# MLA heads' last steps: four gated feature tiles turned in the output bank's free half, out units spread over four steps

## What is computed

```python
o = causal_block_attention(q, k, v).reshape(B, S, E_MLA)   # 16 heads of 128
return (o * jax.nn.silu(g)) @ w_out                        # w_out 2048 x 2048
```

## Time and profile before

| | us |
|---|---|
| runs | 2507.94, 2508.91, 2509.61 |
| median | 2508.91 |
| profiled execution | 2509.81 |
| its span | 2508.0 |
| granted PE clock, mean | 0.998 |

### The profile page before, as it was taken

How to read it: one execution, slowest core, us unless ns; L and a number is a source line. 1 busy time by engine, 2 the same in 40 slices (tenths; PEclk the granted TensorE clock), 3 DMA queues, 4 the chain that set the end, 5 groups by cost and what they waited for, 6 DMA issues and landing times.

```text
span 2508.0 us, 34234 instructions
## 1 busy us (share of the span) xinstructions
PE 2480.3 (99%) x12770; PEld 2119.5 (85%) x12770; DVE 1532.5 (61%) x1820; ACT 1323.8 (53%) x1747; POOL 69.3 (3%) x78
## 2 busy tenths in 40 slices
PE   9999999999999999999999999999999999999998
PEld 8888888888789889778888888887988888888886
DVE  7675757744655555556655655555666667686554
ACT  6444444544656665565755455545555545464443
POOL 0000000010000000010100000100000000000110
PEclk9999999999999999999999999999999999999999
DMA  8666666655556644655675564363566666656663
GB/s 305 194 189 188 184 185 191 204 191 187 166 175 187 185 142 136 217 181 189 185 209 164 143 180 143 104 185 110 156 205 179 189 191 184 187 172 203 195 195 113
DMA packets 234239, 450.64 MB, mean 180 GB/s; under 512 B 15105, under 2 KB 60593, under 8 KB 233100
## 3 DMA queue, kind: packets, MB, share of 16 engines
q1 hardware_dynamic: 230624, 435.94, 56.3%
q0 software_dynamic: 2960, 12.58, 1.5%
q10 hardware_dynamic: 540, 0.60, 0.2%
HBM read 446.35 MB, written 2.69 MB: 179 GB/s over the span
## 4 chain that ended last, share of the span: by engine, by line
PE 97%; DVE 1%; ACT 1%; issue 0%; DMA 0%; SPq 0%; DVEq 0%; ACTq 0%
PE ps L662 23%; PE ps L637 18%; PE ps L639 18%; PE ps L638 18%; PE ps L664 12%; PE ps L595 1%; PE ps L1182 1%; PE ps L1049 0%; PE ps L1170 0%; PE ps L903 0%; PE ps L914 0%; PE ps L915 0%; DVE w_lo L1856 0%; DMA raw<-in_pool_w_in 0%; PE ps L686 0%
## 5 line engine op out<-in xcount | busy, mean ns | idle before, releaser
L1856 DVE TENSOR_TENSOR w_lo<-raw,w_hi 128x1024 fp32r<-128x1024 f32 x852 | 1048.1, 1237 | 743.2 <-ACT w_hi L1249 724.1
L1249 ACT ACTIVATE w_hi<-raw 128x1024 fp32r<-128x1024 f32 x852 | 898.9, 1060 | 940.9 <-PE ps L639 570.9
L662 PE MATMUL ps<-x_hi_lo,w_hi 128*128 128x512 f32 x2336 | 821.3, 394 | 1.7 <-DVE w_lo L1856 1.3
L664 PE MATMUL ps<-x_hi_lo,w_lo 128*128 128x256 f32 x2336 | 660.7, 283 | 0.0
L662 PEld LDWEIGHTS ps<-x_hi_lo,w_hi 128*128 128x128 f32 x2336 | 438.7, 188 | 104.0 <-DVE w_lo L1856 2.3
L637 PE MATMUL ps<-w_hi,x_hi_lo 128*128 128x512 f32 (+3 forms) x1280 | 505.0, 395 | 2.6 <-DVE x_hi_lo L1880 1.3
L639 PE MATMUL ps<-w_hi,x_hi_lo 128*128 128x512 f32 (+3 forms) x1280 | 492.0, 384 | 0.0
L638 PE MATMUL ps<-w_lo,x_hi_lo 128*128 128x512 f32 (+3 forms) x1280 | 491.2, 384 | 0.0
L664 PEld LDWEIGHTS ps<-x_hi_lo,w_lo 128*128 128x128 f32 x2336 | 439.2, 188 | 0.0
L637 PEld LDWEIGHTS ps<-w_hi,x_hi_lo 128*128 128x128 f32 x1280 | 241.1, 188 | 45.3 <-issue 5.2
L639 PEld LDWEIGHTS ps<-w_hi,x_hi_lo 128*128 128x128 f32 x1280 | 240.9, 188 | 43.6
(11 more groups left out here) (344 smaller groups left out, 2148.4 us busy)
## 6 DMA issues: line engine op xcount, KB each, us to landing
raw<-in_w_up SPq DMA_DIRECT2D x160, 512.0 KB, 3.9
raw<-in_pool_w_in SPq DMA_DIRECT2D x128, 512.0 KB, 3.9
raw<-in_w_in SPq DMA_DIRECT2D x96, 480.0 KB, 3.7
raw<-in_w_down SPq DMA_DIRECT2D x76, 512.0 KB, 4.7
raw<-in_pool_w_out SPq DMA_DIRECT2D x64, 512.0 KB, 4.4
raw<-in_ple_w_gate SPq DMA_DIRECT2D x64, 512.0 KB, 3.9
raw<-in_mla_w_in SPq DMA_DIRECT2D x56, 448.0 KB, 3.6
raw<-in_pool_w_group SPq DMA_DIRECT2D x32, 512.0 KB, 4.4
```

The lines of the kernel that those rows point to most:

```text
L662: pe.matmul(bank, w_hi[:, slot, cols], xs[:, k].rearrange("p s n -> p (s n)"), start=k == 0, stop=False, skip_group_check=True)
L664: last = pe.matmul(bank[:, 0:T], w_lo[:, slot, cols], xs[:, k, 0, :], start=False, stop=k == nkt - 1, skip_group_check=True)
L1249: act.activation(w_hi[:, u % RING, :], raw[:, slot, :], ACT.Copy).then_inc(S("w_hi"), 1)
L1856: dve.tensor_tensor(w_lo[:, u % RING, :], raw[:, u % RAW, :], w_hi[:, u % RING, :].bitcast(F32), ALU.subtract)\
```

## The change

Four things change.

- Feature tiles 0 to 3 (groups 0 and 1) are turned one by one, at the end of PE's steps 11 to 14, into the free half of bank O. ACT reads each at the end of its step (semaphore `out_tile_T`), DVE after it (`out_tile`). PE waits for this step's gated head before it turns the tile, and the next step's O matmuls wait for DVE to have read it.
- Out units 0 to 3 stand in PE's steps 15 to 18, one in each, ahead of the O matmuls. Units 0 and 1 wait for the tiles, later ones for groups.
- Groups 2, 3 and 4 are turned in the steps: group 2 in step 16 after the probabilities, group 3 at the end of step 17, group 4 at the end of step 18. Groups 5 and 6 are turned ahead of out unit 4, group 7 ahead of unit 5.
- ACT and DVE prepare a weight unit in each of steps 15 to 18, and it now stands ahead of the group. The loop after the heads begins two groups and two units later.

```diff
@@ PE @@
-            if g == 0:
+            if g == 2:
                 pe.wait_ge(S("at_TE"), HEADS)
-            if g == 1:
+            if g == 3:
                 pe.wait_ge(S("at_L"), HEADS)
-            if g == 2:
+            if g == 4:
                 pe.wait_ge(S("at_PTE"), 4 + HEADS)
-            pe.wait_ge(S("at_done"), 4 + (2 * g + 2 if g < 3 else HEADS))
+            pe.wait_ge(S("at_done"), 4 + (2 * g + 2 if g < 5 else HEADS))
...
-                for g in (3, 4) if k == 4 else (k // 2 + 2,) if 4 < k < 12 else ():
+                for g in {8: (5, 6), 10: (7,)}.get(k, ()):
                     turn(gm, heads_out, g)
-                n = out_first + k // 2
-                pe.wait_ge(S(f"t_free{n % 4}"), n // 4 + 2)
+                if k < 4:
+                    pe.wait_ge(S("out_tile"), k + 2)
+                else:
+                    n = out_first + k // 2 - 2
+                    pe.wait_ge(S(f"t_free{n % 4}"), n // 4 + 2)
...
-                if i in (HEADS, HEADS + 1):
-                    turn(gm, heads_out, i - HEADS)
-                if i == HEADS + 1:
-                    next(out_units)
+                if i == HEADS:
+                    turn(gm, heads_out, 2)
...
                 head_products(min(1, STEP_UNITS[i]))
+                if i >= HEADS - 1:
+                    next(out_units)
                 if i >= 3:
...
                     pe.wait_ge(S("at_done"), 4 + hd)
+                    if OUT_TILES <= i - 1 < OUT_TILES + 4:
+                        pe.wait_ge(S("out_tile"), i - OUT_TILES)
...
                 head_products(max(0, STEP_UNITS[i] - 1))
+                if OUT_TILES <= i < OUT_TILES + 4:
+                    k = i - OUT_TILES
+                    pe.wait_ge(S("at_done"), 4 + i - 2)
+                    for tt in range(2):
+                        last = pe.transpose(O_BANK[:, 256 + tt * 128:384 + tt * 128], gm[:, tt, k * 128:k * 128 + 128], ident)
+                    last.then_inc(S("out_tile_T"), 1)
+                if i in (HEADS + 1, HEADS + 2):
+                    turn(gm, heads_out, i + 2 - HEADS)
             t.add("at", HEADS)
 
         mla_heads()
-        turn(gm, heads_out, 2)
@@ ACT @@
                     last.then_inc(S("at_P"), 1)
+                if i >= HEADS - 1:
+                    hi(1)
                 if i >= HEADS:
-                    group(i - HEADS)
-                if i > HEADS:
-                    hi(1)
+                    group(i + 2 - HEADS)
                 hi(max(0, STEP_UNITS[i] - 1))
+                if OUT_TILES <= i < OUT_TILES + 4:
+                    k = i - OUT_TILES
+                    act.wait_ge(S("out_tile_T"), k + 1)
+                    act.activation(xh[:, k, :], O_BANK[:, 256:512], ACT.Copy).then_inc(S("x_hi"), 1)
@@ DVE @@
                     last.then_inc(S("at_L"), 1)
+                if i >= HEADS - 1:
+                    lo(1)
                 if i >= HEADS:
-                    group(i - HEADS)
-                if i > HEADS:
-                    lo(1)
+                    group(i + 2 - HEADS)
                 lo(max(0, STEP_UNITS[i] - 1))
+                if OUT_TILES <= i < OUT_TILES + 4:
+                    k = i - OUT_TILES
+                    dve.wait_ge(S("x_hi"), t.at("xh", 1))
+                    dve.tensor_tensor(xl[:, k, :], O_BANK[:, 256:512], xh[:, k, :].bitcast(F32), ALU.subtract).then_inc(S("out_tile"), 1)
+                    t.add("xh")
```

More of the change, by code:

```diff
@@ L76 @@
 STEP_UNITS = [2, 3] * 7 + [1] + [0] * 4
+OUT_TILES = 11
 GATE_FIRST = MIN_W - (Q_RANK + KV_RANK - 2 * MIN_W) - ROPE
@@ L1559, in mla_heads @@
         def mla_heads():
-            T_BANK, P_BANK = (TB((t.n["bank"] + b) % 4) for b in (0, 2))
+            T_BANK, P_BANK, O_BANK = (TB((t.n["bank"] + b) % 4) for b in (0, 2, 3))
             for i in range(HEADS + 3):
@@ L1613, in _ @@
         for c in range(NCH):
-            mixer_chunk(chunk(8) if c else first_chunk(early=3, begun=2), 6, c)
+            mixer_chunk(chunk(8) if c else first_chunk(early=5, begun=4), 6, c)
             if c == 0:
@@ L2310, in attention @@
             over_heads(dve, t, parts, step, behind=3, chain=8)
-        first_chunk(early=3, begun=2)
+        first_chunk(early=5, begun=4)
         split_p()
```

## The result

| | median us | runs | lowest to highest | against before |
|---|---|---|---|---|
| before | 2508.39 | 21 | 2507.38 to 2509.61 | |
| after | 2514.36 | 21 | 2511.24 to 2518.14 | 1.0025, 95% interval 1.0019 to 1.0031 |

A forecast was written before the change was run, and what follows sets the result against it. It took TensorE, busy 99% of the span, as the bound, so only its waits and clock count. 2508.91 plus 4.0 of waits plus 1.5 of clock gave 2514.4 us, range 2511.5 to 2516.8.

The forecast's parts named there:

- turns of step 16: PE's turns of Q and K in step 16 wait 0.8 to 0.9 us for ACT's delayed table loads and exponentials.
- out unit 2: In step 17, PE waits 3.0 us for group 2's subtraction, behind logits and a weight unit on DVE.
- out unit 3: In step 18, PE waits 2.2 us for group 3, behind gating and a weight unit on DVE.
- turn of group 5: Just after the steps, PE waits 0.7 us for the last head to be done.
- out unit 4: After the steps, PE waits 1.1 us for group 4's subtraction.
- sum, less 3.8 before: New PE waits of 7.8 us less the 3.8 us present before: 4.0 us longer.
- clock, one fall: TensorE's clock falls once to its lower level near the new pauses, costing 1.5 us; likeliest case, chance 0.35.
- sum of 4.66 us: DVE's path in step 16 from the scores' start through logits, weights and subtraction to PE's start; PE has 1.64 us of work.
- Tiles and O at no cost: Steps 11 to 14: tile turns and following O matmuls cost nothing; step 14 tightest with 0.3 us to spare.
- ACT after step 14: ACT reads the last gate chunk after tile 3, table loads moving too: 7.95 us against PE's 7.05.
- three places named for it: Possible clock falls: scores, turns and 3.0 us wait; O, turns and 2.2 us; O, turns and twice about a microsecond.
- rival without a fall: The clock stays up through the new pauses, only waits count: 2512.9 us, chance 0.32.

The follow-up runs named there:

- first experiment: Changed kernel with VectorE's group subtraction again ahead of the weight unit in steps 16 to 18; 2510.18 us, ratio 1.0006.
- reordered kernel: Changed kernel with DVE's group subtraction before the logits, groups 3 and 4 turned before O, ACT's gate chunk read before tile 3; 2506.57 us, ratio 0.9992.
- half filling: Changed kernel with 6, 4, 1 and 2 unread matmuls in TensorE's pauses; 2512.75 us, and 2511.73 when run again beside the changed kernel.

## Why the prediction was right

It said 2514.4 us; the median is 2514.36. Term by term (the last row from the two profiles near the median):

| wait | predicted | measured |
|---|---|---|
| turns of step 16 | 0.8 to 0.9 | 0.70 |
| out unit 2 | 3.0 | 3.02 |
| out unit 3 | 2.2 | 2.13 |
| turn of group 5 | 0.7 | 0.76 |
| out unit 4 | 1.1 | 0.96 |
| sum, less 3.8 before | 4.0 | 3.8 |
| clock, one fall | 1.5 | 1.54 and 1.55 |

**The queue on DVE.** The sum of 4.66 us from the start of the scores (1016.45) to the out unit (1021.11) held row by row: 1.52 to the logits, then logits and maxima 1.18, weights 1.13, subtraction to start 0.83. Taking the weights from ahead of the subtraction shortened the pause by 1.1 us (first experiment), and putting the subtraction ahead of the logits removed it (reordered kernel). This cause is shown.

**Tiles and O at no cost.** The tile turn at 1005.67 came without a wait, the tile's copy on ACT took 0.39 and DVE's subtraction 0.42. O in steps 15 and 16 no longer waits. POOL's loads came later than forecast (1036.93 for 1021.16 in this slowest execution, 15.8 us where some 9 were said), and nothing on PE waited for them.

**ACT after step 14.** The order and the durations held. ACT's timeline of after beside the earlier trace rows:

```profile
1006.09 0.39 ACT L1599 ACTIVATE x_hi_lo<-ps 128x256 fp32r<-128x256 f32 x1 [2.34 <-PE ps L928]
1006.50 1.28 ACT L1353 ACT_TABLE_LOAD   x1
1007.79 1.16 ACT L1353 ACTIVATE mla_gate<-ps,rstd 128x448 f32<-128x448 f32 x2
...
1009.84 1.28 ACT L1588 ACT_TABLE_LOAD   x1
1011.13 0.40 ACT L1588 ACTIVATE mla_logits<-mla_logits,mla_neg_max 128x128 f32<-128x128 f32 x1
```

Both activations start 0.01 us behind a load of 1.28. With a drain of 1.38 us at each load, as the Trainium skill has it ("ScalarE: Activation LUTs", What ACT_TABLE_LOAD costs), the wait in step 16 would have been above 3 us, by estimate; it was 0.70, so the trace does not agree here either.

**The clock.** The likeliest case was one fall at 1.5 us, and that is what the two profiles near the median show in the steps, in the first of the three places named for it and at that price. Two things were not in it. The falls can be longer than the one of the earlier trace rows: the first of the slowest execution ran on over some 6.8 us, through all of out unit 2 and into O. And their number differs between executions of one kernel: the changed kernel spreads over 6.9 us, the kernel before over 2.2, the half filling over 3.3 and 2.4. The rival without a fall is refuted by three profiles out of three with a fall at the end of the pause of 3.02 us (2.86 idle in the row). The Trainium skill ("TensorE: Matmul & The Clock Gate", Why this matters for your kernels) asks only that pauses longer than about this one be avoided. These profiles do not agree with it, but the pause lies at the edge of what it allows; the fall behind pauses of 0.58 and 0.86 us disagrees more clearly.

**Where it was lucky.** The forecast added 5.5 us to 2508.91, the median of three executions; the median of 21 is 2508.39 and the difference 6.0. A start 0.5 too high and a difference 0.5 too small cancel, so the agreement to 0.1 us is chance; to a microsecond it is not. The terms themselves close between profiles: 3.8 of waits and 1.5 of clock make 5.3, and the two profiles near the median stand 5.4 and 4.7 us above that of before (2515.18 and 2514.54 against 2509.81). Between medians 0.7 is left over. A likely reason, not shown: the profile of before contains the later fall and lies 1.4 above its median, so a common execution of before may well be without it, while all three profiles of the changed kernel have it. No profile of before without it exists to settle this. The same kind of remainder stands with no fall in these steps, in the first experiment: waits of 4.8 us against 3.8 give 1.0 and the medians differ by 2.0.

## What to carry to other kernels

When a unit of work is moved forward to fill a gap, follow its inputs through the queue of every engine that makes them: here the filling needed a subtraction that stood behind the very logits that the step itself produces last, plus the unit's own weights, and each filled gap of 0.7 to 1.5 us became a pause of 2 to 3. Price such a pause with the clock that falls behind it, another 1.5 us on 3.8 in this case, and compare several profiles before taking the number of falls as the kernel's. Two remedies reached the same time here. One is the order of the queues: the operation that the bounding engine waits for goes first on the other engines (2506.57 with four units in the steps). The other is to move only the units whose inputs are ready (2506.70 with two, once ACT's order was mended too).

## What the runs showed of the hardware that was not expected

- A matmul of float32 operands, 128x128 against 256 columns, stands in the trace as two and takes 0.42 us back to back (12 of them 4.99), where a 512-column matmul of the rounded type takes 0.23 to 0.24 (12 of them 2.87).
- With unread matmuls in the pauses the granted clock was 1.00 through the steps in three profiles (in two of them 2.5 us of filling in the pause of 3.0); with the same pauses empty it fell to 0.50 in three profiles of three.
- What a fall costs differs between executions of one kernel whose pauses are the same to 0.02 us: 1.54, 1.55 and 2.76 us of loss behind the same pause (the last with the O behind the out unit).
- A later fall, hundreds of microseconds away from the change, stood in eight of twelve profiles and was worth 1.4 us on average: enough to blur a comparison of medians that differ by a microsecond or two.
